# Context row sums as packed 64x64 blocks on TensorE, and eight of twelve modulation chunks inside the context front

## The chip, the cores and the metric

The kernel runs on 1 core of one Trainium2 chip. The metric is the device time of one execution in microseconds (us), as the median of several runs. TensorE (PE) multiplies, VectorE (DVE) and ScalarE (ACT) do the elementwise work, GpSimd (POOL) issues the indirect gathers, and SyncE (SP) issues most of the other transfers. Each engine works through its own queue in order.

## What is computed

One layer of a diffusion backbone on 256 context tokens and 1024 latent tokens, all in float32. The parts that matter here:

```python
mod_ctx = jax.nn.silu(c_ctx) @ w_mod[l] + b_mod[l]            # 6 x 1024: shift1, scale1, gate1, shift2, scale2, gate2
mod_lat = (jax.nn.silu(c) @ w_mod[l] + b_mod[l])[:, None, :]
...
h = _rmsnorm(x, norm1_g) * (1.0 + scale1) + shift1
m, sf, sb = _mixer(h, latent, sf0, sb0, *mw)                    # GLA scan + conformer convolution
x = x + gate1 * m
h = _rmsnorm(x, norm2_g) * (1.0 + scale2) + shift2
x = x + gate2 * _peer(h, *pw)
...
# _peer: 8 heads x top-16 = 128 experts per token
act = jax.nn.gelu(jnp.einsum('td,thkd->thk', xb, u_tab[ib]), approximate=False)
return jnp.einsum('thk,thkd->td', gb * act, v_tab[ib])
```

The last line is the "row sum": for each token, 128 gathered rows of 1024 numbers, each times its own weight, are added up.

## The kernel before

**Tiles and stages.** Tokens are taken in ten tiles of 128: tiles 0 and 1 are context, 2 to 9 latent. The program first computes the modulation vectors, then runs the front (norm, projections, convolution, scan, output projection, then the query projections and scores of the retrieval) for context, then for latent, and then a main loop over the retrieval of tiles 2 to 9.

**Modulation.** `w_mod` is read in twelve chunks of 2 MB into two buffers. For each, TensorE does 8 matmuls of 128x2 by 128x512 (L568), and VectorE adds the bias (L1091). Every float32 matmul stands in the trace as two records, so a chunk is 16 records. After the twelfth chunk VectorE finishes two rows (L1097), the rows are turned into columns (`modT`, L1100), and only then does SyncE load the first tiles of x (L387). Before those it stores all modulation rows to DRAM and copies the gate rows (L353 to L356).

**Retrieval of the context tiles inside the latent front.** The 2x128 slots of tiles 0 and 1 are worked off in pairs (EC = 2). At 129 numbered places of the latent front, the hooks, every engine calls `early` (on SyncE nothing). The hooks are: 16 in the convolution's projections, 9 in the q/k projections, 16 in the v/g projections, 8 in the layer norm, 8 in the gates, 14 in the scan's states, 10 in the attention, 16 in the output projection, and 16 in each of the two blocks (of four tiles) of query projections, `qf0` and `qf1`. At hook c VectorE does the dot products of pair c (L1253), and ScalarE the gelu, the weights and, for TensorE's pairs, a diagonal matrix of the weights (L826 to L835). TensorE adds pair c at hook c+1: per slot two matmuls of 128x128 by 128x512 into `wide` (L557), which makes 8 records for a pair. A list `by_vector` gives some pairs to VectorE instead, as multiply-adds of 128x1024 on PSUM (L1239), also one hook later: every second pair in the convolution and in v/g, and all of them in the output projection and in both blocks of query projections. That is 126 of 256 slots. POOL gathers the rows into a ring of four buffers, `ring_e`; a buffer comes free when its slot has been added (`used_e`, `used_v`).

**Query projections.** In step hp of a block TensorE does 8 matmuls of 128x512 (L754, `qf`) for step hp, then 4 of 128x128 (L761, `sc`) for step hp-1. Then comes its hook:

```python
for hp in range(HP + 1):
    if hp < HP:    ...  # qf of step hp, L754
    if hp:         ...  # sc of step hp-1, L761
    if hp < HP:
        early(s, f"qf{j}", hp)
```

VectorE waits for the scores of its step hp, copies them out of PSUM (L1526), in the first block picks the top 16 of a key list, and then calls its own hook hp. ScalarE calls its hook hp-1 after it has copied `qf` of hp.

Of the kernel before, what the change touches and what calls it, by code (L numbers as in the profile page):

```python
# [20 lines left out]
ALU = mybir.AluOpType  # L21
# [3 lines left out]
P = 128  # L25
# [24 lines left out]
EARLY = 2 * SLOTS // EC  # L50

# [24 lines left out]
def build(nc, a, counts):  # L76
    with ExitStack() as ctx:
# [43 lines left out]
        def take(words):  # L121
# [43 lines left out]
        modrow = arena[0:2, 3 * D + 8 * MAXL + 8 * MAXL + 4 * MAXL:3 * D + 20 * MAXL + 6 * D]  # L165
        assert 6 * D <= 16 * DV
        bmod = arena[0:2, 3 * D + 8 * MAXL:3 * D + 8 * MAXL + 6 * D]
        grow = arena[0:2, 3 * D + 14 * MAXL:3 * D + 16 * MAXL].rearrange("p (a n) -> p a n", a=2)


        ring_e = [sb(f"ring_e{i}", [P, 2 * D])[:] for i in range(ERING)]
        h2e = [sb(f"h2e{i}", [P, D])[:] for i in range(2)]
        spots = [r[:, i:i + 2 * D] for r in (hreg, creg, greg, vreg, arena[:, WORDS - WSLOTS * D:WORDS])
# [23 lines left out]
        diag_e = [sb(f"diag_e{i}", [P, P])[:] for i in range(ERING)]  # L197
# [7 lines left out]
            "consts", "small_in", "cs_ready", "wmod_in0", "wmod_in1", "mod_rows", "mod_cols", "mod_out",  # L205
# [7 lines left out]
            "used_v", "y_std_done", "pick", "gexp_in", "gexp", "idx_ready", "slot_ok", "dot", "gelu", "weight",  # L213
# [78 lines left out]
        hooks, by_vector, at_hook = {}, [], 0  # L292
        for phase, n, vector in (("conv", 16, (False, True)), ("qk", 9, (False,)), ("vg", 16, (False, True)),
                                 ("ln", 8, (False,)), ("gates", 8, (False,)), ("states", 14, (False,)),
                                 ("attn", 10, (False,)), ("out", 16, (True,)), ("qf0", 16, (True,)), ("qf1", 16, (True,))):
            hooks[phase] = at_hook
            by_vector += (vector * n)[:n]
            at_hook += n
        assert at_hook > EARLY

        def vector_sums(k):

            return k % SLOTS >= EC and by_vector[k // EC]

        def used_e(k):

            return S["used_v" if vector_sums(k) else "used_e"].at(k)
# [29 lines left out]
        def _(sp):  # L337
            sp.dma_start(cvec[:], a["c2"]).then_inc(*S["small_in"].mark("c", 16))
            sp.wait_ge(*S["small_in"].at("c"))
            for i in range(2):  # L340
                sp.dma_start(bmod[i:i + 1, :], a["b_mod"]).then_inc(*S["small_in"].mark(("b", i), 16))
# [23 lines left out]
            for s, (t0, t1) in enumerate(STREAMS):  # L365
# [14 lines left out]
                if s == 0:  # L380
                    sp.wait_ge(*S["modT_ready"].at(0))
# [141 lines left out]
        def _(pe):  # L523
# [21 lines left out]
            def early(s, phase, n):  # L545
# [1132 lines left out]
```

## Time and profile before

| | us |
|---|---|
| median of 3 runs | 4428.79 |
| runs | 4423.98, 4428.79, 4439.44 |
| span of the profiled execution, first to last instruction | 4415.7 |
| TensorE busy in it | 3419.6 |
| VectorE busy | 2883.5 |
| ScalarE busy | 887.3 |
| POOL busy | 1498.4 |

The profiled execution has no device time of its own in the results; its span is 4415.7 us, 13.1 us under the median of the runs, and those 13.1 us lie around the span (start and end of the program). The mean granted TensorE clock is 0.899 of full speed. Busy time of TensorE is modelled, since matmuls overlap; the distance between starts of rows is the better measure.

### The profile page before, as it was taken

The page shows a single profiled execution, that of the slowest core. Times are in us where ns is not written, and L with a number is a line of the kernel's source. Part 1 is how long each engine was busy: PE and PEld are TensorE (multiplying, and loading weights), DVE is VectorE, ACT ScalarE, POOL GpSimd, SP SyncE. Part 2 cuts the span into 40 slices and gives each one's busy share as a digit, 9 for nine tenths or more (in the row PEclk, how much of TensorE's full clock was granted, in tenths as well). Part 3 has the DMA queues.
Part 4 walks back from the last instruction along what each step waited for, and adds up shares of the span by engine and source line. Part 5 has one row for each costly group of instructions (what it writes and reads, how often), then busy time and mean ns, then how long its engine had stood idle before and what let it go on. Part 6 is the DMA issues. An engine that isn't in the chain of part 4 may idle for free.

```text
span 4415.7 us, 33544 instructions
## 1 busy us (share of the span) xinstructions
PE 3419.6 (77%) x7972; PEld 1528.7 (35%) x7972; DVE 2883.5 (65%) x6259; ACT 887.3 (20%) x2429; POOL 1498.4 (34%) x1297
## 2 busy tenths in 40 slices
PE   7767799976788886777787777777777677777777
PEld 1536344333443443233232333332333233333332
DVE  0535897847556877775775775774775774775774
ACT  0131321454322112111111111111111111111111
POOL 0000222212222223444454354344344444444343
PEclk9878899987898988889988899899899989898899
DMA  6324666756677788999999999999999999999997
GB/s 232 121 85 155 221 231 220 283 197 218 228 282 284 288 325 322 421 421 421 421 421 421 420 414 421 408 409 420 412 406 421 412 404 420 404 411 421 414 408 293
DMA packets 223619, 1494.71 MB, mean 338 GB/s; under 512 B 25388, under 2 KB 26668, under 8 KB 56660
## 3 DMA queue, kind: packets, MB, share of 16 engines
q0 software_dynamic: 184752, 1344.36, 75.7%
q1 hardware_dynamic: 37256, 143.43, 8.7%
q10 hardware_dynamic: 1440, 5.24, 0.3%
q14 instruction: 137, 1.12, 0.1%
q8 instruction: 34, 0.56, 0.0%
HBM read 1466.93 MB, written 26.02 MB: 338 GB/s over the span
## 4 chain that ended last, share of the span: by engine, by line
DMA 46%; PE 26%; DVE 10%; issue 9%; POOL 4%; ACT 3%; SPq 1%; POOLq 0%; DVEq 0%; ACTq 0%; PEldq 0%
DMA arena<-in_uv,idx 29%; DMA ring_e<-in_uv,idx 13%; PE wide L777 5%; PE bank L754 4%; PE bank L597 4%; PE bank L620 3%; PE wide L557 3%; POOL arena L516 3%; PE bank L737 3%; DMA arena<-in_w_q 2%; DVE ring_e L1253 2%; PE bank L568 1%; POOL ring_e L516 1%; PE bank L647 1%; DMA arena<-in_w_mod 1%
## 5 line engine op out<-in xcount | busy, mean ns | idle before, releaser
L777 PE MATMUL wide<-arena 128*128 128x512 f32 x3072 | 1521.6, 653 | 486.2 <-ACT arena L1032 464.0
L1564 DVE CUSTOM_DVE_ANT_0 arena<-arena,h2e 128x1024 f32<-128x1024 f32 x768 | 927.1, 1224 | 535.9 <-DMA arena<-in_uv,idx 511.8
L516 POOL DMA_INDIRECT arena<-in_uv,idx x768 | 900.7, 1173 | 1081.1 <-PE wide L777 918.9
L777 PEld LDWEIGHTS wide<-arena 128*128 128x128 f32 x3072 | 626.0, 209 | 1378.5 <-issue 767.7
L501 POOL DMA_INDIRECT ring_e<-in_uv,idx x256 | 306.0, 1195 | 1076.4 <-PE wide L557 516.3
L777 PE MATMUL wide<-ring_e,arena 128*128 128x512 f32 x1024 | 510.5, 656 | 162.3 <-ACT arena L1032 162.3
L1032 ACT ACTIVATE arena<-ident,small 128x128 f32<-128x128 f32 x1024 | 327.5, 390 | 623.2 <-DVE small L1571 609.5
L1564 DVE CUSTOM_DVE_ANT_0 ring_e<-ring_e,h2e 128x1024 f32<-128x1024 f32 x256 | 309.0, 1224 | 183.4 <-DMA ring_e<-in_uv,idx 183.0
L1253 DVE CUSTOM_DVE_ANT_0 ring_e<-ring_e,h2e 128x1024 f32<-128x1024 f32 x256 | 307.6, 1221 | 171.8 <-DMA ring_e<-in_uv,idx 171.2
L516 POOL DMA_INDIRECT ring_e<-in_uv,idx x256 | 287.0, 1121 | 375.5 <-PE wide L777 326.0
L777 PEld LDWEIGHTS wide<-ring_e,arena 128*128 128x128 f32 x1024 | 209.2, 210 | 463.4 <-issue 248.3
L1029 ACT ACTIVATE small<-small 128x4 f32<-128x4 f32 x256 | 52.6, 206 | 1566.7 <-DVE small L1564 1566.7
L754 PE MATMUL bank<-arena 128*128 128x512 f32 (+1 forms) x768 | 302.2, 550 | 44.0 <-DMA arena<-in_w_q 41.5
L557 PE MATMUL wide<-ring_e,diag_e 128*128 128x512 f32 x520 | 273.4, 675 | 71.4 <-ACT diag_e L835 71.3
L597 PE MATMUL bank<-arena 128*128 128x512 f32 (+3 forms) x624 | 228.1, 524 | 11.3 <-issue 9.8
L754 PEld LDWEIGHTS bank<-arena 128*128 128x128 f32 x768 | 151.3, 202 | 170.5 <-issue 118.6
L557 PEld LDWEIGHTS wide<-ring_e,diag_e 128*128 128x128 f32 x520 | 110.1, 218 | 214.5 <-issue 141.5
L1239 DVE SCALAR_TENSOR_TENSOR wide<-ring_e,wts_e,wide 128x1024 f32<-128x1024 f32 x126 | 161.7, 1284 | 2.2
L597 PEld LDWEIGHTS bank<-arena 128*128 128x128 f32 (+1 forms) x624 | 115.0, 185 | 121.5 <-issue 113.2
L737 PE MATMUL bank<-arena 128*128 128x512 f32 x320 | 143.2, 608 | 13.6 <-DMA arena<-in_w_out 12.9
L1348 DVE SCALAR_TENSOR_TENSOR arena<-arena,cw 128x255 f32<-128x255 f32 (+29 forms) x240 | 152.3, 705 | 0.0
L620 PE MATMUL bank<-arena 128*128 128x512 f32 x320 | 141.1, 599 | 4.7 <-DMA arena<-in_w_vg 4.7
(180 smaller groups left out, 2413.6 us busy)
## 6 DMA issues: line engine op xcount, KB each, us to landing
arena<-in_w_mod SPq DMA_DIRECT2D x12, 2048.0 KB, 7.8
arena<-in_w_q SPq DMA_DIRECT2D x48, 512.0 KB, 10.4
arena<-in_w_cols SPq DMA_DIRECT2D x24, 512.0 KB, 3.9
arena<-in_uv,idx POOLq DMA_INDIRECT x768
arena<-in_x SPq DMA_DIRECT2D x20, 512.0 KB, 3.7
sc_d<-arena SPq DMA_DIRECT2D x36, 256.0 KB
arena<-in_w_vg SPq DMA_DIRECT2D x16, 512.0 KB, 4.2
arena<-in_w_out SPq DMA_DIRECT2D x16, 512.0 KB, 5.6
```

The source lines that it names most:

```text
L501: pool.indirect_dma_start(out=ring_e[k % ERING], out_offset=None, in_=a["uv"], in_offset=bass.IndirectOffsetOnAxis(ap=idx[k // SLOTS][:, k ...
L516: pool.indirect_dma_start(out=ring[k % RING], out_offset=None, in_=a["uv"], in_offset=bass.IndirectOffsetOnAxis(ap=idx[p][:, k:k + 1], axis=0)
L557: ins = pe.matmul(wide[k // SLOTS][:, h * 512:(h + 1) * 512], lhsT=diag_e[k % ERING], rhs=ring_e[k % ERING][:, D + h * 512:D + (h + 1) * 512],
L597: ins = pe.matmul(bk[0:M, 0:n * P], lhsT=w[:, k * M:(k + 1) * M], rhs=hT[:, k, cols_], start=(k == 0), stop=(k == KD - 1))
L620: ins = pe.matmul(bk[:], lhsT=hT[:, k, (t - t0) * P:(t - t0 + 1) * P], rhs=w[:, (k % 2) * 512:(k % 2 + 1) * 512], start=(k == 0), stop=(k ...
L737: ins = pe.matmul(bk[:], lhsT=l, rhs=w[:, (k % 2) * 512:(k % 2 + 1) * 512], start=(k == 0), stop=(k == KD - 1))
L754: ins = pe.matmul(bk[:, 0:n * P], lhsT=w[:, k * P:(k + 1) * P], rhs=H2T[:, k, 0:n * P], start=(k == 0), stop=(k == KD - 1))
L777: ins = pe.matmul(wide[p][:, c * 512:(c + 1) * 512], lhsT=diag[r], rhs=ring[r][:, D + c * 512:D + (c + 1) * 512], start=(first and r == 0) ...
L1032: act.activation(diag[r], ident[:], ACT.Copy, scale=wts[:, r:r + 1]).then_inc(S["diag_ready"].sem, 1)
L1239: dve.scalar_tensor_tensor(out=wide[t_][:], in0=ring_e[r_][:, D:2 * D], scalar=wts_e[:, r_:r_ + 1], in1=wide[t_][:], op0=ALU.mult, op1=ALU ...
L1253: dve.tensor_tensor_reduce(out=ring_e[r_][:, 0:D], in0=ring_e[r_][:, 0:D], in1=h2e[k // SLOTS], scale=1.0, scalar=0.0, op0=ALU.mult, op1=A ...
L1564: dve.tensor_tensor_reduce(out=ring[r][:, 0:D], in0=ring[r][:, 0:D], in1=h2b[p], scale=1.0, scalar=0.0, op0=ALU.mult, op1=ALU.add, accum_o ...
```

## The change

The twelve chunks become four ahead of the context front and eight inside it: `modulate(n)` on TensorE and `modulated(n)` on VectorE, with chunks 4 and 5 ahead of the gates, 6 to 9 one in each of the four gate units, and 10 and 11 in the two scan steps. They are loaded by POOL into the memory of `ring_e`, which is free then. In the retrieval of the context tiles `by_vector` and VectorE's sums are gone. All 128 pairs are TensorE's, each as 8 matmuls of 64x64 by 64x512: row half r of both slots goes to `wide[r]`, slot j of the pair to partitions 64j to 64j+63. After each tile's last pair the halves are brought together (`swap_halves` on ScalarE, `fold_halves` on VectorE).

```diff
+HALF = P // 2
+MODS, FIRST_MODS = 12, 4
...
-        def used_e(k):
-            return S["used_v" if vector_sums(k) else "used_e"].at(k)
+        def used_e(k):
+            return S["used_e"].at(k // EC)
...
-            for n in range(12):
+            for n in range(FIRST_MODS):
                 if n >= 2:
                     sp.wait_ge(*S["bank_full"].at(("mod", n - 2)))
                 sp.dma_start(wmod[n % 2], a["w_mod"][n]).then_inc(*S[f"wmod_in{n % 2}"].mark(n, 16))
-            sp.wait_ge(*S["mod_rows"].at("a2"))
-            sp.dma_start(mod_d, modrow).then_inc(*S["mod_out"].mark("rows", 16))
-            sp.wait_ge(*S["mod_out"].at("rows"))
...
+            def load_mod(n):
+                c = slice(n * 512, (n + 1) * 512)
+                pool.wait_ge(*S["bank_full"].at(("mod", n - 2)))
+                pool.dma_start(wmod_late[n % 2], a["w_mod"][n]).then_inc(*S[f"wmod_late{n % 2}"].mark(n, 16))
+                pool.wait_ge(*S["bank_dve"].at(("mod", n - 2)))
...
+            for n in range(FIRST_MODS, FIRST_MODS + 2):
+                load_mod(n)
+            for n in range(FIRST_MODS, MODS):
+                pool.wait_ge(*S["mod_rows"].at(n))
+                pool.dma_start(mod_d[:, n * 512:(n + 1) * 512], row_late[n % 2]).then_inc(*S[f"mod_late{n % 2}"].mark(n, 16))
+                if n + 2 < MODS:
+                    load_mod(n + 2)
...
                 c = hook(s, phase, n) - 1
                 if not 0 <= c < EARLY:
                     return
-                for k in range(EC * c, EC * c + EC):
-                    if vector_sums(k):
-                        continue
-                    if k % SLOTS and vector_sums(k - 1):
-                        pe.wait_ge(*used_e(k - 1))
-                    pe.wait_ge(*S["diag_e"].at(k))
-                    for h in range(2):
-                        ins = pe.matmul(wide[k // SLOTS][:, h * 512:(h + 1) * 512], lhsT=diag_e[k % ERING],
-                                        rhs=ring_e[k % ERING][:, D + h * 512:D + (h + 1) * 512],
-                                        start=(k % SLOTS == 0), stop=(k % SLOTS == SLOTS - 1), skip_group_check=True)
-                    ins.then_inc(*S["used_e"].mark(k))
+                k = EC * c
+                if k == SLOTS:
+                    pe.wait_ge(*S["folded"].at((0, 1)))
+                pe.wait_ge(*S["diag_e"].at(k + EC - 1))
+                for h in range(2):
+                    for o in range(2):
+                        for r in range(2):
+                            j = k + (r + o) % 2
+                            rows, to = slice(r * HALF, (r + 1) * HALF), slice((j - k) * HALF, (j - k + 1) * HALF)
+                            ins = pe.matmul(wide[r][to, h * 512:(h + 1) * 512], lhsT=diag_e[j % ERING][rows, :],
+                                            rhs=ring_e[j % ERING][rows, D + h * 512:D + (h + 1) * 512],
+                                            start=(k % SLOTS == 0), stop=(k % SLOTS == SLOTS - EC),
+                                            skip_group_check=True)
+                ins.then_inc(*S["used_e"].mark(c))
...
+            def swap_halves(t):
+                act.wait_ge(*used_e((t + 1) * SLOTS - 1))
+                for h in range(2):
+                    hc = slice(h * 512, (h + 1) * 512)
+                    if t or h:
+                        act.wait_ge(*S["folded"].at((t, 0) if h else (t - 1, 1)))
+                    act.activation(swap[0:HALF, :], wide[0][HALF:P, hc], ACT.Copy)
+                    act.activation(swap[HALF:P, :], wide[1][0:HALF, hc], ACT.Copy).then_inc(*S["swap_in"].mark((t, h)))
...
                 c = hook(s, phase, n)
                 if c >= 0:
-                    early_sums(c - 1)
                     early_dots(c)
+                for t in range(2):
+                    if c == (t + 1) * SLOTS // EC:
+                        fold_halves(t)
```

Three places of the engines' queues, in the order of the program (no time is in these rows). The first is TensorE in the context front, from the last convolution product to the attention. L684 is the old L647, L698 the old L658 (gates), L715 and L722 the old L673 and L680 (scan steps), L602 the modulation. Before:

```order
L647 MATMUL bank<-arena 128x256 x16
L658 MATMUL bank<-arena,wup 128x256 x4
L673 MATMUL bank<-ident,arena 128x128 x4
L680 MATMUL bank<-arena 128x256 x4
L673 MATMUL bank<-ident,arena 128x128 x4
L680 MATMUL bank<-arena 128x256 x4
```

Now:

```order
L684 MATMUL bank<-arena 128x256 x16
L602 MATMUL bank<-ring_e,csil 2x512 x16
L698 MATMUL bank<-arena,wup 128x256
L602 MATMUL bank<-ring_e,csil 2x512 x8
L698 MATMUL bank<-arena,wup 128x256
L602 MATMUL bank<-ring_e,csil 2x512 x8
L698 MATMUL bank<-arena,wup 128x256
L602 MATMUL bank<-ring_e,csil 2x512 x8
L698 MATMUL bank<-arena,wup 128x256
L602 MATMUL bank<-ring_e,csil 2x512 x8
L715 MATMUL bank<-ident,arena 128x128 x4
```

Each gate matmul after the first now stands behind a modulation chunk, and so does the first row of the scan.

The second place is TensorE in the query projections of the latent blocks (L798 and L805 are the old L754 and L761). Before:

```order
L754 MATMUL bank<-arena 128x512 x8
L761 MATMUL bank<-arena 128x128 x4
L754 MATMUL bank<-arena 128x512 x8
L761 MATMUL bank<-arena 128x128 x4
L754 MATMUL bank<-arena 128x512 x8
```

Now:

```order
L798 MATMUL bank<-arena 128x512 x8
L805 MATMUL bank<-arena 128x128 x4
L588 MATMUL wide<-ring_e,diag_e 64x512 x8
L798 MATMUL bank<-arena 128x512 x8
L805 MATMUL bank<-arena 128x128 x4
L588 MATMUL wide<-ring_e,diag_e 64x512 x8
```

The packed sums of a pair (L588) now stand between the scores of one step and the projection of the next but one.

The third is VectorE in the same steps, first block: copy of the scores, copy of the own tile, top 16, then the hook. Before:

```order
L1526 COPY arena<-bank 128x4x128
L1531 COPY arena<-arena 128x128
L1126 MAX sv<-arena 128x8
L1128 MAX_INDEX si<-sv,arena 128x8
L1130 MATCH_REPLACE arena<-sv,arena 128x128
L1132 MAX sv<-arena 128x8
L1134 MAX_INDEX si<-sv,arena 128x8
L1239 SCALAR_TENSOR_TENSOR wide<-ring_e,wts_e,wide 128x1024 x2
L1253 ISA ring_e,dots_e<-ring_e,h2e 128x1024
```

Now:

```order
L1610 COPY arena<-bank 128x4x128
L1615 COPY arena<-arena 128x128
L1200 MAX sv<-arena 128x8
L1202 MAX_INDEX si<-sv,arena 128x8
L1204 MATCH_REPLACE arena<-sv,arena 128x128
L1206 MAX sv<-arena 128x8
L1208 MAX_INDEX si<-sv,arena 128x8
L1330 ISA ring_e,dots_e<-ring_e,h2e 128x1024
```

The two multiply-adds of L1239 are gone from ahead of the dot products.

## Rows read from the trace of the kernel before

**Rows 1.** Page, busy tenths of the DMA engines in 40 slices.

```profile
DMA  6324666756677788999999999999999999999997
```

**Rows 2.** Windows: length, busy PE, PEld, DVE, ACT, POOL, granted clock, DMA share, GB/s.

```profile
470.00:860.00 390.00, 378.19 (x872) 164.03 (x873) 317.63 (x554) 103.95 (x240) 104.65 (x84) 0.98 0.68 247
860.00:1259.00 399.00, 295.64 (x798) 147.01 (x797) 220.89 (x458) 173.28 (x423) 83.51 (x81) 0.83 0.62 223
1259.00:1390.00 131.00, 118.06 (x278) 51.79 (x276) 97.37 (x126) 21.73 (x64) 39.06 (x31) 0.97 0.77 293
1390.00:1562.00 172.00, 137.90 (x420) 71.39 (x420) 130.38 (x264) 25.96 (x76) 40.93 (x33) 0.90 0.78 288
1562.00:1735.00 173.00, 136.95 (x400) 69.37 (x400) 130.52 (x218) 25.16 (x72) 42.89 (x34) 0.89 0.83 315
```

**Rows 3.** Timeline of TensorE in the modulation (start, length, line, count, idle before).

```profile
33.05 13.96 PE L568 MATMUL bank<-arena,csil 128*2 128x512 f32 x32 [1.08 <-DMA arena<-in_w_mod]
47.97 12.61 PE L568 MATMUL bank<-arena,csil 128*2 128x512 f32 x29 [0.96 <-DMA arena<-in_w_mod]
```

**Rows 4.** Timeline after the last modulation chunk, to the first load of x.

```profile
111.11 0.19 DVE L1100 COPY modT<-wide 128x32 f32<-128x32 f32 x1 [1.24 <-PE wide L575]
...
114.25 0.90 SPq L387 DMA_DIRECT2D arena<-in_x  x2
```

**Rows 5.** Timeline of TensorE in the context front, gates to scan.

```profile
229.28 1.99 PE L658 MATMUL bank<-arena,wup 32*128 32x256 f32 x8
257.15 1.12 PE L673 MATMUL bank<-ident,arena 128*128 128x128 f32 x4 [25.88 <-DVE arena L1417]
...
270.37 5.17 PE L720 MATMUL bank<-arena 64*128 64x128 f32 x32 [0.83 <-DVE arena L1455]
```

**Rows 6.** Page, DMA issues of `w_mod`: count, KB each, us to landing.

```profile
arena<-in_w_mod SPq DMA_DIRECT2D x12, 2048.0 KB, 7.8
```

**Rows 7.** TensorE: a pair's row sums at full clock, and after a wait.

```profile
504.90 3.60 PE L557 MATMUL wide<-ring_e,diag_e 128*128 128x512 f32 x8
...
1066.05 6.15 PE L557 MATMUL wide<-ring_e,diag_e 128*128 128x512 f32 x8 [5.12 <-ACT diag_e L835]
```

**Rows 8.** TensorE in the attention: products of 64 rows, then of 128 rows.

```profile
1155.25 1.26 PE L720 MATMUL bank<-arena 64*128 64x128 f32 x16
1156.52 1.13 PE L693 MATMUL bank<-arena 128*128 128x128 f32 x8
```

**Rows 9.** VectorE, first unit of the output projection.

```profile
1278.71 0.69 DVE L1501 TENSOR_TENSOR arena<-bank,arena 128x512 f32<-128x512 f32 x1 [15.95 <-DMA arena<-mod_d]
```

**Rows 10.** TensorE in the first latent block of query projections.

```profile
1407.90 16.18 PE L754 MATMUL bank<-arena 128*128 128x512 f32 x32 [0.83 <-issue]
...
1431.68 1.05 PE L761 MATMUL bank<-arena 128*128 128x128 f32 x8
1432.57 7.03 PE L754 MATMUL bank<-arena 128*128 128x512 f32 x16
...
1463.88 8.65 PE L754 MATMUL bank<-arena 128*128 128x512 f32 x16 [7.87 <-DMA arena<-in_w_q]
...
1554.11 1.16 PE L761 MATMUL bank<-arena 128*128 128x128 f32 x8 [1.95 <-ACT arena L1019]
```

**Rows 11.** VectorE after a step's scores: first block, then second block.

```profile
1432.77 0.69 DVE L1526 COPY arena<-bank 128x512 f32<-128x512 f32 x1 [2.01 <-PE bank L761]
...
1435.36 2.59 DVE L1239 SCALAR_TENSOR_TENSOR wide<-ring_e,wts_e,wide 128x1024 f32<-128x1024 f32 x2
...
1440.15 0.08 DVE L1253 DVE_READ_ACCUMULATOR2_ANT dots_e<- 128x1 f32 x1
...
1689.16 0.69 DVE L1526 COPY arena<-bank 128x512 f32<-128x512 f32 x1 [1.20 <-PE bank L761]
```

**Rows 12.** ScalarE from the dot products to the diagonal matrices.

```profile
1064.99 0.20 ACT L826 ACTIVATE gel_e<-dots_e 128x2 f32<-128x2 f32 x1 [8.72 <-DVE dots_e L1253]
...
1065.62 0.68 ACT L835 ACTIVATE diag_e<-ident,wts_e 128x128 f32<-128x128 f32 x2
```

More of the change, by code:

```diff
@@ L196, in build @@
         idx = [sb(f"idx{i}", [P, SLOTS], U32) for i in range(2)]
-        diag_e = [sb(f"diag_e{i}", [P, P])[:] for i in range(ERING)]
+        diag_e = [sb(f"diag_e{i}", [P, HALF])[:] for i in range(ERING)]
+        ident_h = sb("ident_h", [P, HALF])
+        swap = sb("swap", [P, 512])[:]
         dots_e, gel_e, wts_e = (sb(n, [P, ERING])[:] for n in ("dots_e", "gel_e", "wts_e"))
@@ L287, in by_head @@
             return r.rearrange("p (a o n) -> p a o n", o=2, n=P)[:, :, odd, :]
[L292 to L295, printed above, removed]
+        hooks, at_hook = {}, 0
+        for phase, n in (("conv", 16), ("qk", 9), ("vg", 16), ("ln", 8), ("gates", 8), ("states", 14), ("attn", 10),
+                         ("out", 16), ("qf0", 16), ("qf1", 16)):
             hooks[phase] = at_hook
-            by_vector += (vector * n)[:n]
             at_hook += n
         assert at_hook > EARLY
-        def vector_sums(k):
-            return k % SLOTS >= EC and by_vector[k // EC]
         def used_e(k):
-            return S["used_v" if vector_sums(k) else "used_e"].at(k)
+            return S["used_e"].at(k // EC)
         def hook(s, phase, n):
@@ L408, in _ @@
                     sp.dma_start(X1[:, t - t0, :], a["x"][t * P:(t + 1) * P, :]).then_inc(*S["x1_in"].mark(s, 16))
+                for i in range(2):
+                    sp.wait_ge(*S[f"mod_late{i}"].at(8 + i))
                 for dst, row in ((gate1b, 2), (shift2b, 3), (a2b, 4)):
@@ L562, in _, with modulate @@
+                ins.then_inc(*S["used_e"].mark(c))
             pe.wait_ge(*S["consts"].at("all"))
             pe.wait_ge(*S["cs_ready"].at(0))
-            for n in range(12):
+            def modulate(n):
                 bk = bank(("mod", n))
-                pe.wait_ge(*S[f"wmod_in{n % 2}"].at(n))
+                late = n >= FIRST_MODS
+                pe.wait_ge(*S[f"wmod_{'late' if late else 'in'}{n % 2}"].at(n))
                 for k in range(KD):
-                    ins = pe.matmul(bk[0:2, :], lhsT=csil[:, k, :], rhs=wmod[n % 2][:, k, :],
+                    ins = pe.matmul(bk[0:2, :], lhsT=csil[:, k, :], rhs=(wmod_late if late else wmod)[n % 2][:, k, :],
@@ L569, in _ @@
                                     start=(k == 0), stop=(k == KD - 1))
                 full(ins, ("mod", n))
-            pe.wait_ge(*S["mod_rows"].at("a2"))
+            for n in range(FIRST_MODS):
+                modulate(n)
+            pe.wait_ge(*S["mod_rows"].at("a1"))
             for which in range(2):
@@ L830, in early @@
                                    scale=gate[t_][:, g0 + j:g0 + j + 1]).then_inc(*S["weight_e"].mark(k0 + j))
-                for j in range(0 if vector_sums(k0) else EC):
+                for j in range(EC):
                     act.wait_ge(*S["weight_e"].at(k0 + j))
@@ L1087, in _ @@
             dve.wait_ge(*S["consts"].at("all"))
+            dve.tensor_tensor(ident_h[:], ident[:, 0:HALF], ident[:, HALF:P], ALU.add).then_inc(*S["consts"].mark("half"))
             dve.wait_ge(*S["small_in"].at("all"))
-            for n in range(12):
+            for n in range(FIRST_MODS):
                 bk = wait_full(("mod", n))
```

120 lines of the change are left out of this document (85 added, 35 removed).

## The prediction

> **What bounds the kernel now.** I read the slices of the page first. From the eighteenth on the DMA engines stand at nine tenths [rows 1]: the main loop is bound by the gathers, nothing in the change touches it, and a microsecond gained or lost ahead of it is one gained or lost at the end. So the question is the 1740 us before.
>
> Next the windows by stage. From 470 to 860 (latent convolution, q/k and v/g projections) TensorE is busy 378 of 390 us at a clock of 0.98: it is the bound [rows 2]. From 860 to 1259 (norm, gates, scan, attention) it is busy 296 of 399 at 0.83, with waits that run through all engines. From 1259 to 1390 (output projection) it is nearly full again, and in the two blocks of query projections, 172 and 173 us long, it has 35 us idle in each, VectorE 42. In the modulation TensorE and a 2 MB load take turns: the chunks start 14.92 us apart per two, 7.46 each [rows 3]. The gates of the context front are the reverse: TensorE stands idle for 25.9 us [rows 5].
>
> **The change, part one: modulation.** Eight chunks leave the head: 8 x 7.46 = 59.7 us. SyncE no longer stores the rows ahead of x; between `modT` and the first load of x lie 2.95 us [rows 4], which go too. Chunk 5 (2 MB) is on its way when x is loaded; I charge 2 us. That is -61.
>
> The eight chunks come back between 229 and 270 us, 41 us that held 8 gate products and the scan [rows 5]. Each is 6.9 us of TensorE (13.96 for two, rows 3), 55 in all. If they only filled TensorE's idle time there, the stretch would grow by some 55 - 26 - 3 = 26 us. But in its queue each gate product stands behind a chunk, and chunk n+2 is loaded only after POOL has seen chunk n's row: 6.9 of matmul, 1.1 of VectorE and 1 of POOL (my estimates), 7.8 of landing [rows 6] is 17 us on each of two buffers, 8.5 a chunk. Chunks 4 and 5 find their weights waiting (13.8 us), the other six take 9 with the gate products between them (54), the rest of the scan 4: 72, so +31. With the lower clock after such gaps (below, 1.6 a gap, at worst in all six) +41. I take +36. Net of part one: **-25**, bounds -35 and -18.
>
> **Part two: the row sums.** A pair costs TensorE 3.43 us today (8 records, 3.60 with the tail, rows 7). Now it is 16 records of a quarter each. One after another they would take 6.9 us; the size hangs on how many run side by side. What the trace shows: 16 records on halves of 64 rows took 1.27 us from their start to the next product's, 79 ns each, while 8 records on all 128 rows took 1.13 us, 141 with the tail [rows 8]. So row halves do run side by side, in float32. For output halves no row exists: between 2 at once (3.43) and 4 at once (1.72). I take four, and 0.2 us a pair for switching: 1.9.
>
> The Trainium skill (TensorEngine Tiling (Array Packing), Tiling Modes) has four independent 64x64 tiles, and says that changing the mode drains the engine. By the first the pair would cost 1.7 us; the second speaks against small packets between full-size ones, two switches a pair. No row prices a drain; in rows 8 the engine goes from 64-row to 128-row products without an idle time in the listing.
>
> By stage, 1.9 against 3.43 where TensorE had the pair, against none where VectorE had it:
> - Convolution and v/g: 32 pairs x 1.9 - 16 x 3.43 = +6; VectorE's relief there saves perhaps 5. +1.
> - q/k: 9 x -1.5 = -14.
> - Norm, gates, scan, attention: 40 pairs, all TensorE's before. In the attention and half of the norm the sum lies on the path: 13 x -1.5 = -20. In gates and scan the path is a circle of gather, dots, weights and sums; both buffers now come free together, so of 1.5 (more at the low clock) half remains: 22 x -0.6 = -13. One fold in the scan, four passes on each side: +4. Together -29.
> - Output projection: 15 pairs x 1.9 = +28 on an engine that is 118 of 131 us busy. Also a new wait: hook 1 now needs the dots of a pair which VectorE does after its first unit, and that starts at 1278.7, late by a 16 us wait for a broadcast [rows 9]. TensorE, which ran ahead before, loses about 9 + 1.6; 4 are won back in later waits for weights. +34.
>
> Sum without the query projections: **-8**.
>
> **Part three: what the packed sums wait for in the query projections.** This decides. In step hp+1 TensorE does `qf` of hp+1, the scores of hp, then the sums of pair hp (the order in the front's second place). VectorE does the dots of pair hp only after it has copied the scores of hp (third place). So the sums stand directly behind the scores on which, through VectorE and ScalarE, they wait. Before, TensorE had no sums here and ran on. Now each of 15 steps in each block is a circle:
> - `qf` 6.9 (7.03 with tail) and scores 0.9 [rows 10];
> - VectorE, first block: the scores end at 1432.73, the dots at 1440.23, less 2.6 of multiply-adds that are gone: 4.9. Second block: the copy 0.7 and the dots 2.3 alone: 3.0 [rows 11];
> - ScalarE: from gelu's start 1064.99 to the second diagonal 1066.30, with the hand-overs 1.4 [rows 12];
> - the sums 1.9; a norm of a tile in four hooks of the first block, two more passes of 1.25: 0.65 on average;
> - the clock: after an idle time of 7.87 us `qf` took 8.65 and not 7.03 [rows 10], and a pair's sums after 5.12 us took 6.15 and not 3.60 [rows 7]. I charge the smaller, 1.6, per step.
>
> First block 6.9 + 0.9 + 4.9 + 1.4 + 1.9 + 0.65 + 1.6 = 18.2; second 15.7. Gathers don't prolong it: two circles lie between a buffer's release and its next dots. What is queued behind the waiting sums is the next `qf`, so ScalarE, VectorE and SyncE's score stores all wait with it. First block: 8 + 15 x 18.2 + 1 = 282, against 1555.3 - 1407.9 = 147 now: +135. Second: 8 + 15 x 15.7 + 1 = 244 against some 150: +93. **+228**; without any clock loss +180.
>
> The Trainium skill (TensorE: Matmul & The Clock Gate, Loop structure matters more than you think) says that idle gaps between bursts of matmuls leave the engine at half clock; the rows just named agree (+1.6 and +2.6 us).
>
> **Sum.** -25 - 8 + 228 = +195. The profiled span 4415.7 becomes 4611; with the 13.1 us around it, which bring it to the median of 4428.8, **4624**.
>
> **Rivals.**
> - *Only row halves run side by side.* A pair costs 3.6. +1.7 for 41 pairs in the TensorE-bound stages (70), some 20 in norm to attention, 26 in the output projection, 52 in the circles: +168, so 4792. For it: only row halves have a row. Against it: nothing in the trace. 0.18.
> - *The circles cost less*: clock kept up, the context front at its lower bound, the scan gains more. The sum goes to +195 - 48 - 10 - 20 = +117: 4546. 0.10.
> - *The change is faster.* The wait for dots would have to be covered, that is, VectorE would have to be done with a pair before TensorE reaches its sums. The 35 us idle and the waits for w_q speak for some slack in these blocks; but the dots' place behind the scores forbids it. If it were so, a step costs 6.9 + 0.9 + 1.9 = 9.7, as long as now (147 / 15 = 9.8), and -33 remains: 4396. It decides from a wait of under some 1 us per step. 0.06.
> - *No packing at all*: records one after another, 6.9 a pair. Over +500: beyond 4950. Rows 8 speak against it. 0.04.
>
> **Chances and range.** Forecast 0.62, its own range 4560 to 4690 (a clock loss between 0.8 and 2.6 a step, part one's bounds, 1.7 to 2.4 a pair). With the rivals on both sides the range is 4510 to 4800. A measurement tells about 0.3% (13 us) from no change: faster 0.06, the same 0.02, slower 0.92.
>
> **What would show it.** The first load of x near 51 us and the context attention near 245 rather than 270. Sums of a pair in about 1.9 us from start to next product, in the convolution; 3.5 there means the row-halves rival. In the query projections a wait of TensorE's sums for ScalarE's diagonals of some 6 us in the first block and 4 in the second, 30 times, blocks of some 300 and 265 us, and a clock under 0.85 there. If TensorE shows no such waits, the prediction is wrong in sign.

## The result, and the profile after

The changed kernel takes **4656.97 us** (median of 4 runs, 4654.2 to 4658.03) against 4429.6 for the kernel before on the same chip (4423.98 to 4439.44): a ratio of **1.0516, 95% interval 1.0501 to 1.053**, 227 us slower. The forecast was 4624, its range 4510 to 4800.

The page of the profile after, row for row against [rows 1]: busy tenths of the DMA engines in 40 slices. They stand at nine from the eighteenth slice on, before from the seventeenth (the prediction counted one too many), and a slice is 116.4 us instead of 110.4. The main loop from its first product on TensorE to the end is as long as it was: 2667.8 us against 2665.8.

```profile
DMA  5344766656565354499999999999999999999997
```

The windows by stage, with the columns of [rows 2]. The first is the latent convolution with the q/k, v and g projections, the second norm to attention, then the output projection, then the two blocks of query projections.

```profile
438.00:822.00 384.00, 376.19 (x1308) 144.12 (x1312) 277.94 (x518) 107.02 (x267) 96.14 (x83) 0.98 0.69 249
822.00:1231.00 409.00, 244.42 (x1132) 109.82 (x1124) 224.51 (x465) 172.72 (x433) 83.49 (x80) 0.76 0.59 219
1231.00:1390.00 159.00, 147.33 (x500) 57.07 (x496) 64.47 (x101) 29.47 (x97) 34.47 (x32) 0.95 0.65 246
1402.00:1700.00 298.00, 193.52 (x656) 81.73 (x656) 83.41 (x223) 27.01 (x91) 29.96 (x32) 0.79 0.43 155
1700.00:1985.00 285.00, 206.10 (x656) 87.93 (x656) 96.44 (x191) 39.51 (x112) 33.37 (x35) 0.79 0.54 199
```

Read the last two against 172 and 173 us in [rows 2]. No engine is busy for more than 73% of them, the busy share of the DMA engines fell from 0.78 and 0.83 to 0.43 and 0.54, and the granted clock from 0.90 to 0.79. A stage in which every engine idles more and which is longer than before points to a circle of waits. Its timeline on TensorE, one step of each block (in each row start, length, line, count, and in brackets the idle time before and who ended it):

```profile
1473.87 1.05 PE L805 MATMUL bank<-arena 128*128 128x128 f32 x8
1481.18 3.31 PE L588 MATMUL wide<-ring_e,diag_e 64*64 64x512 f32 x16 [6.26 <-ACT diag_e L893]
1484.42 7.13 PE L798 MATMUL bank<-arena 128*128 128x512 f32 x16
1491.39 1.05 PE L805 MATMUL bank<-arena 128*128 128x128 f32 x8
1498.70 3.69 PE L588 MATMUL wide<-ring_e,diag_e 64*64 64x512 f32 x16 [6.26 <-ACT diag_e L893]
...
1748.26 3.69 PE L588 MATMUL wide<-ring_e,diag_e 64*64 64x512 f32 x16 [4.29 <-ACT diag_e L893]
1751.88 7.98 PE L798 MATMUL bank<-arena 128*128 128x512 f32 x16
1759.70 1.05 PE L805 MATMUL bank<-arena 128*128 128x128 f32 x8
1765.05 3.69 PE L588 MATMUL wide<-ring_e,diag_e 64*64 64x512 f32 x16 [4.29 <-ACT diag_e L893]
```

The scores product (L805) ends, TensorE stands for 6.26 or 4.29 us until ScalarE's diagonals come, does the sums (L588), and only then the next projection (L798). In the four steps of the first block in which VectorE also norms a tile it stands for 8.7 to 8.9 us. The diagonals wait for VectorE, here in a step of the second block:

```profile
1744.01 0.69 DVE L1610 COPY arena<-bank 128x512 f32<-128x512 f32 x1 [13.54 <-PE bank L805]
1744.62 1.22 DVE L1330 CUSTOM_DVE_ANT_0 ring_e<-ring_e,h2e 128x1024 f32<-128x1024 f32 x1
...
1746.90 0.08 DVE L1330 DVE_READ_ACCUMULATOR2_ANT dots_e<- 128x1 f32 x1
```

and then ScalarE:

```profile
1747.02 0.20 ACT L884 ACTIVATE gel_e<-dots_e 128x2 f32<-128x2 f32 x1 [3.31 <-DVE dots_e L1330]
1747.26 0.48 ACT L887 ACTIVATE wts_e<-gel_e,gate 128x1 f32<-128x1 f32 x2
1747.64 0.57 ACT L893 ACTIVATE diag_e<-ident_h,wts_e 128x64 f32<-128x64 f32 x2
```

VectorE starts when the scores are there and has been idle for 13.54 us; the diagonals are done 4.2 us after it started. No engine is slow; each waits for the one before it.

A pair of packed sums at full clock, to hold against [rows 7], and the context front, to hold against [rows 4, 5]:

```profile
456.31 1.95 PE L588 MATMUL wide<-ring_e,diag_e 64*64 64x512 f32 x16 [1.57 <-ACT diag_e L893]
458.19 7.13 PE L634 MATMUL bank<-arena 128*128 128x512 f32 x16
```

```profile
202.28 7.03 PE L602 MATMUL bank<-ring_e,csil 128*2 128x512 f32 x16 [1.60 <-DMA ring_e<-in_w_mod]
...
225.18 8.35 PE L602 MATMUL bank<-ring_e,csil 128*2 128x512 f32 x16 [5.36 <-DVE arena L1537]
...
245.37 2.79 PE L764 MATMUL bank<-arena 64*128 64x128 f32 x32
```

The pair takes 1.88 us from its start to the next product's, and the context attention starts at 245.37 where it started at 270.37.

### The profile page after: what moved, and what is told of

It is laid out like the page before. It is cut to its first block, busy times and chain, and to the rows that moved or that the text cites. A ratio compares the mean times of both kernels' runs of the same rounds, so it can differ in the third digit from the quotient of the medians.

```text
span 4656.3 us, 36647 instructions
## 1 busy us (share of the span) xinstructions
PE 3536.2 (76%) x9500; PEld 1508.8 (32%) x9500; DVE 2734.1 (59%) x6143; ACT 915.8 (20%) x2563; POOL 1472.7 (32%) x1333
## 4 chain that ended last, share of the span: by engine, by line
DMA 42%; PE 32%; DVE 10%; issue 9%; POOL 4%; ACT 3%; SPq 0%; POOLq 0%; DVEq 0%; ACTq 0%
DMA ring_e<-in_uv,idx 21%; DMA arena<-in_uv,idx 18%; PE bank L798 6%; PE wide L822 6%; PE wide L588 5%; PE bank L634 4%; PE bank L657 3%; PE bank L781 3%; DVE ring_e L1330 2%; POOL ring_e L545 2%; POOL arena L545 2%; PE bank L602 1%; PE bank L684 1%; PE bank L805 1%; DMA arena<-mod_d 1%
## 5 line engine op out<-in xcount | busy, mean ns | idle before, releaser
L822 PE MATMUL wide<-arena 128*128 128x512 f32 x3072 | 1540.6, 660 | 479.1 <-ACT arena L1092 476.0
L545 POOL DMA_INDIRECT arena<-in_uv,idx x768 | 885.8, 1153 | 1132.6 <-PE wide L822 950.0
L530 POOL DMA_INDIRECT ring_e<-in_uv,idx x256 | 271.9, 1062 | 1356.0 <-PE wide L588 1184.7
L588 PE MATMUL wide<-ring_e,diag_e 64*64 64x512 f32 x2048 | 334.2, 780 | 275.0 <-ACT diag_e L893 270.3
L545 POOL DMA_INDIRECT ring_e<-in_uv,idx x256 | 291.9, 1140 | 357.3 <-PE wide L822 272.2
L822 PEld LDWEIGHTS wide<-ring_e,arena 128*128 128x128 f32 x1024 | 208.1, 209 | 445.0 <-issue 252.4
L798 PE MATMUL bank<-arena 128*128 128x512 f32 (+1 forms) x768 | 312.7, 563 | 7.9 <-DMA arena<-in_w_q 6.3
L1610 DVE COPY arena<-bank 128x512 f32<-128x512 f32 (+1 forms) x48 | 28.9, 602 | 432.1 <-PE bank L805 432.1
L588 PEld LDWEIGHTS wide<-ring_e,diag_e 64*64 64x64 f32 x2048 | 79.6, 163 | 450.0 <-ACT diag_e L893 293.8
L798 PEld LDWEIGHTS bank<-arena 128*128 128x128 f32 x768 | 154.3, 207 | 182.9 <-issue 171.0
L781 PE MATMUL bank<-arena 128*128 128x512 f32 x320 | 149.7, 624 | 7.5 <-DMA arena<-in_w_out 6.8
L657 PE MATMUL bank<-arena 128*128 128x512 f32 x320 | 145.5, 609 | 6.6 <-DMA arena<-in_w_vg 6.6
```

What stands on the lines that cost most here:

```text
L530: pool.indirect_dma_start(out=ring_e[k % ERING], out_offset=None, in_=a["uv"], in_offset=bass.IndirectOffsetOnAxis(ap=idx[k // SLOTS][:, k ...
L545: pool.indirect_dma_start(out=ring[k % RING], out_offset=None, in_=a["uv"], in_offset=bass.IndirectOffsetOnAxis(ap=idx[p][:, k:k + 1], axis=0)
L588: ins = pe.matmul(wide[r][to, h * 512:(h + 1) * 512], lhsT=diag_e[j % ERING][rows, :], rhs=ring_e[j % ERING][rows, D + h * 512:D + (h + 1) ...
L657: ins = pe.matmul(bk[:], lhsT=hT[:, k, (t - t0) * P:(t - t0 + 1) * P], rhs=w[:, (k % 2) * 512:(k % 2 + 1) * 512], start=(k == 0), stop=(k ...
L781: ins = pe.matmul(bk[:], lhsT=l, rhs=w[:, (k % 2) * 512:(k % 2 + 1) * 512], start=(k == 0), stop=(k == KD - 1))
L798: ins = pe.matmul(bk[:, 0:n * P], lhsT=w[:, k * P:(k + 1) * P], rhs=H2T[:, k, 0:n * P], start=(k == 0), stop=(k == KD - 1))
```

## The experiments

All changes are small edits of the kernel before or of the changed kernel. To place them, this table has the profiled length of each stretch less that of the kernel before, in us (a stretch runs from the first product of one stage on TensorE to the first of the next; before, these starts were 470.4, 952.8, 1259.4, 1407.9 and 1750.0). The runs were made on several chips, and with each the kernel before was measured on the same chip: 4429.6 us with the changed kernel, 4429.86 with e1 to e3, 4422.62 with e5 to e8, 4427.15 with e9 to e11. The last column has the median less that one; where two runs differ by some 10 us, go by it.

| kernel | ahead of the latent convolution | convolution to norm | gates to attention | output projection | query projections | median us | less before |
|---|---|---|---|---|---|---|---|
| changed kernel | -31.7 | -6.0 | +9.3 | +22.7 | +244.2 | 4656.97 | +227.4 |
| e1, modulation only | -24.2 | -0.1 | +3.7 | -1.6 | +4.0 | 4401.96 | -27.9 |
| e2, packing only | -2.0 | -6.5 | +8.0 | +19.3 | +244.2 | 4684.28 | +254.4 |
| e3, sums ahead of scores | -25.9 | -7.7 | +8.8 | +20.1 | +42.2 | 4454.54 | +24.7 |
| e5, second tile unpacked | -17.4 | -10.3 | +6.6 | -0.6 | +12.9 | 4405.35 | -17.3 |
| e6, eight filler products | -26.6 | -10.1 | +9.2 | +20.1 | +215.6 | 4628.77 | +206.2 |
| e7, no sums from norm to attention | -27.2 | -13.0 | -5.6 | +21.1 | +245.5 | 4640.62 | +218.0 |
| e8, half the products (one run) | -17.1 | -7.2 | +9.3 | +19.4 | +267.9 | 4694.36 | +271.7 |
| e9, four filler products | -27.5 | -11.1 | +8.0 | +17.4 | +187.2 | 4594.16 | +167.0 |
| e10, dots ahead of scores | -30.2 | -8.0 | +8.5 | +17.5 | +39.6 | 4444.23 | +17.1 |
| e11, unpacked in the query projections | -27.2 | -1.4 | +3.8 | -1.6 | +274.8 | 4663.0 | +235.9 |

The first column shows how far single executions scatter: all these kernels but e2 have the same context front. All differences are to one profiled execution of the kernel before, and that was a quick one (below).

**e1, the modulation moved alone.** The diff's modulation part on the kernel before.

> The modulation chunks move, the row sums stay as before. Theory: the move gives what the kernel with both showed up to the first latent convolution, 31.7 us, and nothing later takes it back: 4398 us, between 4392 and 4406. Rival: the chunks that now lie in the context front cost latent stages too (writes, waits of the queues), and part of the loss of the full change is theirs: above 4410 us.

Measured: 4401.96 us, ratio 0.9939 (0.9922 to 0.9957), 27.9 us faster. As the theory had it; nothing behind the convolution takes it back.

**e2, the packing alone.** The rest of the diff; all twelve chunks are ahead.

> The row sums are packed, all twelve modulation chunks stay ahead. Theory: the two parts don't touch each other, so the time is that of the full change plus 31 us: 4688 us, between 4680 and 4696. Rival: the parts share something (the late chunks lie in the gathers' buffers), and the sum of the two single effects misses the full one by more than 10 us.

Measured: 4684.28 us, ratio 1.0581 (1.0563 to 1.0599), 254.4 us slower than the kernel before. -27.9 and +254.4 make +226.5; both together measured +227.1 against the same runs of before (4656.97 - 4429.86). The parts add up, and the whole loss is the packing's.

**e3, the sums ahead of the scores product.**

```
                             full(ins, ("qf", b, hp))
                         if hp:
+                            early(s, f"qf{j}", hp - 1)
                             pe.wait_ge(*S["bank_act"].at(("qf", b, hp - 1)))
...
-                        if hp < HP:
-                            early(s, f"qf{j}", hp)
```

> Full change, but in the query projections TensorE does a pair's sums ahead of the scores product of that step, so that the dot products and diagonals have a whole projection (7 us at full clock) to get ready. Theory of the circle: a step falls to projection 7.0 + sums 1.9 + scores 1.1 = 10.2 us from 18.6 and 17.1, both blocks lose 240 us together, 4657 falls to 4417 us (4405 to 4450). Rival one, it is the clock and the amount of work on TensorE and not the circle: the steps stay above 15 us, over 4600 us. Rival two, the gathers are late because their buffers come free late: the buffers come free no earlier here, VectorE then waits for them, and steps stay near 13 us, about 4510 us.

Measured: 4454.54 us, ratio 1.0055 (1.0037 to 1.0074): one moved line gives back 202 us. TensorE's timeline, with sums in L588 and scores in L806:

```profile
1427.00 1.95 PE L588 MATMUL wide<-ring_e,diag_e 64*64 64x512 f32 x16
1428.88 1.16 PE L806 MATMUL bank<-arena 128*128 128x128 f32 x8
1429.88 7.03 PE L798 MATMUL bank<-arena 128*128 128x512 f32 x16
1436.84 1.95 PE L588 MATMUL wide<-ring_e,diag_e 64*64 64x512 f32 x16
...
1653.97 8.83 PE L798 MATMUL bank<-arena 128*128 128x512 f32 x16 [3.04 <-DMA arena<-in_w_q]
```

A step is 9.84 us without a gap, and the window from 1402 to 1580 is at clock 0.97. Over both blocks the sums wait 16.7 us in all (166.9 in the changed kernel) and 13.5 go to weights that come late. It is 37 us above the 4417 expected; those waits, which I had left out, are 30 of them. The first rival (above 4600) is out. The second (13 us a step) is out too, since the step is 9.84 though the buffers come free no earlier.

**e10, the dots ahead of the scores' copy.** The other place where the circle can be cut, on VectorE, with TensorE's order as in the changed kernel.

```
                     for hp in range(HP):
+                        early(s, f"qf{j}", hp)
                         bk = wait_full(("sc", b, hp))
...
-                        early(s, f"qf{j}", hp)
                         if b < 2 and hp == HP - 1:
```

> Full change, but in the query projections VectorE does a step's dot products ahead of the copy of its scores; TensorE's order stays. Theory of the circle: it breaks here as well, since the dot products no longer follow scores: what is left between projection and sums is ScalarE's copy, gelu, weights and diagonals (0.6 + 0.2 + 0.5 + 0.6 us) beside 1.0 us of scores. Steps of 11.2 us, 4448 us (4430 to 4470). Rival, it is TensorE's place for the sums alone that counts (what run e3 changed): steps stay over 15 us, above 4600 us.

Measured: 4444.23 us, ratio 1.004 (1.0029 to 1.0051). TensorE in the first block:

```profile
1457.21 1.05 PE L805 MATMUL bank<-arena 128*128 128x128 f32 x8
1459.15 1.95 PE L588 MATMUL wide<-ring_e,diag_e 64*64 64x512 f32 x16 [0.88 <-ACT diag_e L893]
1461.02 7.13 PE L798 MATMUL bank<-arena 128*128 128x512 f32 x16
```

The wait is 0.88 us, the step 10.8, and the clock is up again (0.98 from 1402 to 1690), though TensorE does the very instructions of the changed kernel in their order. So it isn't TensorE's place for the sums alone that counts: the circle opens as well where VectorE's dots no longer stand behind the scores.

**e11, the same circle without packing.** On e1, one line of the table of hooks: in `qf0` and `qf1` VectorE's sums go to TensorE as full-size products.

```
-  ("out", 16, (True,)), ("qf0", 16, (True,)), ("qf1", 16, (True,))
+  ("out", 16, (True,)), ("qf0", 16, (False,)), ("qf1", 16, (False,))
```

> Base is run e1 (modulation moved, sums unpacked); only the query projections' sums leave VectorE and go to TensorE, as full-size products of 128x128 by 512. Theory: the loss comes from where the sums are done and not from the packed form; the circle closes here too and each step is 1.6 to 3.3 us longer than in the full change, since a pair takes 3.5 us at full clock and up to 7: 4402 + 244 + 31 x 2.2 = 4715 us (4690 to 4750). Rival: the packed form closes the circle (its one wait for both diagonals of a pair); with a wait for each diagonal the first products start earlier and only TensorE's work is added: 4402 + 31 x 3 = 4500 us.

Measured: 4663.0 us, ratio 1.0534 (1.0506 to 1.0561), 261 us above e1. TensorE in the second block:

```profile
1757.72 7.03 PE L798 MATMUL bank<-arena 128*128 128x512 f32 x16
1764.59 1.05 PE L805 MATMUL bank<-arena 128*128 128x128 f32 x8
1769.75 5.25 PE L589 MATMUL wide<-ring_e,diag_e 128*128 128x512 f32 x8 [4.11 <-ACT diag_e L879]
```

The wait is 4.11 us where it was 4.29, so the packed form doesn't make the circle; the sums' move from VectorE does. It came out 52 us below the 4715 expected: I had added 1.6 to 3.3 us a step, and the step is 17.2 us against 16.8 here, in the first block 20.6 against 19.1 on average. The full-size sums take 5.1 us to the next product instead of 3.6, but behind them the projection runs at full speed (7.03 against 7.98). So in this stage packing saves about 31 us (+274.8 against +244.2) of a loss that it didn't cause.

**e6 and e9, products that only fill the wait.** In TensorE's queue, between the scores and the sums, eight (e6) or four (e9) further products of 128x512 into the next free bank; they are overwritten.

```
+                        if s == 1 and 0 < hp < HP:
+                            pe.wait_ge(*emptied(units[-4]))
+                            for k in range(KD):
+                                pe.matmul(banks[len(units) % 4][:, 0:n * P], lhsT=ident[:], rhs=H2T[:, k, 0:n * P],
+                                          start=(k == 0), stop=(k == KD - 1))
```

> Full change, and in the query projections TensorE does eight further products of 128x512 (3.5 us at full clock) into the next free bank after each step's scores product, in the time in which it waits for the diagonals; their result is overwritten. Theory: what the wait adds beside itself is clock (sums 3.7 us instead of 1.9, projection 7.1 to 8.3 instead of 7.0). With the wait filled the clock stays at full: 2.8 us less for each of 31 steps, 4570 us (4550 to 4600). Rival: the clock has another cause: the products only add work, 4657 us where the wait hides them (4.3 us of wait for 3.5 us of work) and up to 4700 us where they run at the half clock.

> As run e6, but four further products of 128x512 instead of eight: run e6's profile shows that its eight took 7.0 us (16 records), 2.7 us more than the wait of the second block. Theory of the clock: four take 3.5 us and lie wholly inside the wait of 4.3 and 6.3 us; if the clock still stays at full, a step of the second block is 1.0 + 4.3 + 1.9 + 7.0 = 14.2 us instead of 16.7 in e6 and one of the first about 16.2: 4580 us (4570 to 4600). Rival: less filling doesn't hold the clock, and the time falls back towards the full change: 4630 to 4660 us.

Measured: e6 4628.77 us, ratio 1.0465 (1.0446 to 1.0485); e9 4594.16, ratio 1.0379 (1.0353 to 1.0405). Useless work makes the changed kernel 28 and 63 us faster by the medians, 21 and 60 by the last column of the table. TensorE in e9's second block (fillers in L811):

```profile
1760.46 1.05 PE L805 MATMUL bank<-arena 128*128 128x128 f32 x8
1761.35 3.60 PE L811 MATMUL bank<-arena,ident 128*128 128x512 f32 x8
1765.80 1.95 PE L588 MATMUL wide<-ring_e,diag_e 64*64 64x512 f32 x16 [0.86 <-ACT diag_e L898]
1767.68 7.13 PE L798 MATMUL bank<-arena 128*128 128x512 f32 x16
```

and in e6's:

```profile
1751.30 7.03 PE L811 MATMUL bank<-arena,ident 128*128 128x512 f32 x16
1758.26 1.95 PE L588 MATMUL wide<-ring_e,diag_e 64*64 64x512 f32 x16
```

The granted clock of the second block is 0.95 (e9, 1700 to 1960) and 0.97 (e6, 1700 to 1985) against 0.79. The sums are back at 1.88 and the projection at 6.97. In e9's second block the step is the 14.2 us expected. The total is 14 us above the 4580 expected, and the first block has the step that is off: 17.9 us on average and not 16.2, with waits of 5.3 to 5.5 us in its four steps with a norm and sums of 3.69 behind such a wait. My price for e6's eight products was wrong: 16 records take 7.0 us, not 3.5, more than the wait; that is why it missed its 4570. e9 gives the clock's share of the circle: at least 57 of the 244 us of the query projections.

**e8, half the products.** The lower 64 rows are left out.

```
-                        for r in range(2):
+                        for r in range(2 if k % SLOTS in (0, SLOTS - EC) else 1):
```

> Full change without the products of the lower 64 rows of the diagonals and gathered tiles (eight of sixteen products in a pair stay), so the sums lack half their terms. Theory, four products at once (two row halves by two column halves): the two column halves of the upper rows still run side by side, the pair takes the same 1.9 us. Rival, a 64x64 product is by itself cheaper and they run one after another: half the time, 0.95 us.

Measured, one run: 4694.36 us. TensorE:

```profile
488.54 1.93 PE L588 MATMUL wide<-ring_e,diag_e 64*64 64x512 f32 x8
490.40 7.13 PE L634 MATMUL bank<-arena 128*128 128x512 f32 x16
```

Eight records take 1.86 us as sixteen took 1.88: in the whole kernel four run side by side, here two. The single time lies above the changed kernel's; in the query projections the mean projection record took 700 ns instead of 649, with half the sums done. That is a single run, and it leaves the reason open.

**e7, no sums from norm to attention.**

```
+                if phase in ("ln", "gates", "states", "attn") and k % SLOTS not in (0, SLOTS - EC):
+                    pe.matmul(wide[0][0:HALF, 0:HALF], lhsT=diag_e[k % ERING][0:HALF, :],
+                              rhs=ring_e[k % ERING][0:HALF, D:D + HALF], start=False, stop=False,
+                              skip_group_check=True).then_inc(*S["used_e"].mark(c))
+                    return
```

> Full change without the packed products of the pairs that lie in the norm, gates, scan and attention stages: one product of 64 columns is left of sixteen of 512 in each, so the outputs lack these rows. Theory: in these stages TensorE waits for ScalarE and VectorE, and its sums lie in those waits, so that neither halving them (the change) nor removing them gains: the stages together stay within 8 us of the full change's 408 us, the kernel within 10 us of 4657 us. Rival, TensorE's time counts there and packing costs something that hid its gain: 39 pairs by 1.9 us and more, 4580 us or less.

Measured: 4640.62 us, ratio 1.05 (1.0478 to 1.0521). That is 16 us below the changed kernel by the medians and 9 by the last column, and the two intervals overlap (1.0501 to 1.053), so the times alone don't separate the kernels. The profile does: the stages take 385.3 us (828.2 to 1213.5) against 408.3, 23 us less, of which 8 in the norm and 16 in the scan; the other kernels with both tiles packed lie within 4 us of the changed one there. So neither expectation holds as put: more than 8 us in the stages, and far from the rival's 77. The waits explain most of it. The groups of TensorE's sums from norm to attention, of the changed kernel (822 to 1231; busy and mean ns, idle before):

```profile
L588 PE MATMUL wide<-ring_e,diag_e 64*64 64x512 f32 x648 | 109.7, 806 | 94.7 <-ACT diag_e L893 90.0 <-DVE h2e L1316 4.7
```

and of the kernel before (860 to 1259):

```profile
L557 PE MATMUL wide<-ring_e,diag_e 128*128 128x512 f32 x314 | 179.1, 723 | 60.5 <-ACT diag_e L835 60.4
```

and, in e7's window of the same stages, the length, the engines' busy times, the granted clock and the DMA share, as in [rows 2]:

```profile
828.00:1213.00 385.00, 178.78 (x594) 105.72 (x590) 222.95 (x464) 171.77 (x433) 86.09 (x80) 0.63 0.62 229
```

The packing took 69 us off TensorE's sums, and 34 of them came back as waits ahead of the sums themselves; 17 more are waits for VectorE ahead of the first products of the attention (L764, 19.0 us against 2.5). e7 took a further 87 us off the sums (109.7 to 22.6), and 23 of them came out. So most of the sums' time lies in waits, but not all of it. In the norm the wait for ScalarE's squares and for its activation grew from 4.80 and 6.22 us to 5.64 and 7.78 (before, at 868.7 and 884.2; after, at 834.0 and 849.7), with the norm as long as it was (92.4 us against 92.5). And the granted clock fell from 0.83 to 0.76, and to 0.63 in e7, where TensorE has still less to do.

**e5, the second tile unpacked.** The first tile's sums packed, the second's with full-size products and VectorE's multiply-adds as in the kernel before. A first form of it, e4 (expected at 4392 us, its rival at 4400 to 4420), needed more on-chip memory than is left beside the full-size diagonals and has no time; e5 lays a small tile into `swap` to make room. The edit:

```
+            return k >= SLOTS + EC and by_vector[k // EC]
...
+                if k >= SLOTS:
+                    for k in range(EC * c, EC * c + EC):
+                        if vector_sums(k):
+                            continue
```

> Full change, but only the first tile's 128 sums are packed (pairs 0 to 63, up to the scan); the second tile has the full-size products and VectorE's multiply-adds of the kernel before. Theory: the loss belongs to the sums that left VectorE in the output and query projections. What is left is the modulation's 27.9 us (run e1) and what the packed front gained up to the scan in the stage times of run e2, 5.8 us: 4396 us (4388 to 4404). Rival: the fold of the two halves, which lies in the scan here as there, or the full-size diagonals take that gain back: 4400 to 4415 us.

Measured: 4405.35 us, ratio 0.996 (0.9947 to 0.9973). With VectorE's sums back, 245 of the 255 us between the changed kernel and e1 are gone by the last column of the table (252 by the medians), though half the sums are still packed. The time is 1 us outside the theory's range and inside the rival's, and its interval overlaps e1's (0.9922 to 0.9957): in the whole kernel no gain of the packed first tile over e1 can be measured. In its stage there is one: from the convolution to the norm every kernel with a packed first tile lies at -6.0 to -13.0 in the table, and the two without (e1, e11) at -0.1 and -1.4. In e5 it is lost again behind the attention, with +12.9 in the query projections against e1's +4.0. The best kernel measured is e1, the modulation alone.

## Why the prediction was right, and where it was off

- **Part one, the modulation: right.** -25 forecast; e1 measured -27.9, inside the bounds of -35 to -18 (the sum's own upper end, -61 + 41, is -20). x is loaded at 49.85 and the context attention starts at 245.37, as forecast. Chunks waited for weights only 2.27 and 1.60 us; the last two stood behind VectorE's states (5.36 and 2.04), which I hadn't named.
- **A pair's price: right.** 1.9 forecast with four at once, 1.88 measured, and e8 shows that it is four at once. The 1.88 rules out the rival of row halves alone (3.6 a pair) and that of no packing (6.9). The 0.2 us for switching was about the difference to 1.72; whether it is a switch or the tail of the last product no run tells. The Trainium skill (TensorEngine Tiling (Array Packing), Tiling Modes) has four independent 64x64 tiles, and these runs agree; of the drain that it names for a change of mode they show at most those 0.16 us.
- **Convolution to g: about right.** -13 forecast (+1 and -14), -5.8 in the profile (438.7 to 822.7 against 470.4 to 860.3). In v and g the stage grew by 6 us (147.5 against 141.5), since TensorE, which got VectorE's sums, was the bound (144 of 147 us): VectorE's relief gave nothing there.
- **Norm to attention: the step that failed.** "Together -29"; it is +9.2 in the profile (822.7 to 1231.0 against 860.3 to 1259.4). I took TensorE's sums to lie on the path in half of these stages. For the most part they lie in its waits for ScalarE and VectorE: less work there turned into more wait and a lower clock. With almost no sums left (e7) the stages are 23 us shorter than with packed ones, and 14 shorter than before. The fold was near its +4: TensorE waited 4.7 us for it. Of the +9.2, 4 aren't the packing's: e1, without it, has +4.2 in the same stages.
- **Output projection: right in kind, too high.** +34 forecast, +22.7 measured, +17.4 to +20.1 in e3, e9 and e10. The new wait in its first unit is there, 8.93 us at 1256.21 where 9 was forecast.
- **Query projections: the cause right, a term too small.** +228 forecast, +244 measured. The first block took 294 us from its first product to its last (282 forecast), the second 267 (244); together they grew by 260 us, of which 16 were won back between and behind the blocks. The circle is shown: e3 and e10 cut it at two different places, and each gives back over 200 us (202 and 205 in the table); e11 closes it without packing. The waits were forecast at about 6 and 4, and are 6.26 (8.7 to 8.9 with a norm) and 4.29, 30 of them and 166.9 us in all. The mis-sized term is the clock at 1.6 us a step. The sums took 114.0 us in 32 pairs instead of 32 x 1.88 = 60, and the projections 252.4 instead of e10's 233.1: 73 us in 30 steps, 2.4 a step. I had the loss fall on the sums or on the projection; it falls on both. The Trainium skill (TensorE: Matmul & The Clock Gate, Loop structure matters more than you think) has the half clock come from idle gaps; e9 agrees, since products in the gap bring the clock back (0.79 to 0.95).
- **The sum.** -25 - 8 + 228 was +195 in the profiled span; it is +241. The 46 us are 38 in norm to attention, 16 in the query projections, 7 up to g and 2 behind them, less 7 in the context front and 11 in the output projection; one is rounding. The 13.1 us around the span were wrong too: the changed kernel's profiled execution has a span of 4656.3 and a time of 4658.03, 1.7 us more. The profiled execution of before was a quick one, and the 13.1 us were mostly the scatter between executions; they hid 11 us of the miss. That the time fell inside the forecast's own range of 4560 to 4690 is owed in part to luck: one stage had the wrong sign, and 18 us of misses the other way (context front and output projection) and those 11 stood against it.
- **The rival "faster".** Its condition, a wait under 1 us a step, is met in e3 and e10, and they are still slower than before, by 0.55% and 0.4%. Its price was wrong in two places: the -33 has the -29 of norm to attention in it, which didn't come, and "147 / 15 = 9.8" divides a stretch of 16 projections by 15. Before, a step took 9.2 us; with the sums TensorE's work alone fills 9.84 (e3), and some waits for weights (13.5 us in e3) are left.

## What to carry to other kernels

When work moves from one engine to another, ask first what the instruction will stand behind in the new queue, and whether that is the same thing on which its own inputs wait; here the sums cost 244 us in the query projections behind the scores and 42 one place earlier. In a stage where the engine that gets faster mostly waits for others, write its gain down as small or nought and look at what the new idle time does to its clock. Measure the two halves of a combined change apart: the small one (27.9 us gained) was hidden under the large one (254.4 lost).

## What the hardware showed beyond what was expected

- Four 64x64 products with 512 columns in float32 ran side by side: 16 records in 1.88 us, 117 ns each, against 429 ns for a full-size record. Packets of these between full-size products left no gap in the listing.
- Gaps of 4.3 us (second block) and 6.3 to 8.9 us (first) on TensorE in each step of 17 to 21 cost another 2.4 us a step in slower products behind them. Filling them in part with useless products brought the granted clock of the second block from 0.79 to 0.95 and made the kernel 60 us faster (e9).
- Less work for TensorE in the same stages lowered the clock there in steps: 0.83 with full-size sums, 0.76 with packed ones, 0.63 with almost none (e7).
- Kernels with the same context front reached the latent convolution between 438.7 and 453.3 us in their profiled executions. A single profile tells no difference under some 15 us there; what makes it is open.
